# mLSTM mixer of a streaming encoder: normalisers as rows from 32-wide column tiles, the four old-state products of a head in one group, query copy ahead of decay

## The chip, the cores and the metric

One Trainium2 chip, one of its cores. TensorE (PE) multiplies, with its weight loads shown apart as PEld; VectorE (DVE) and ScalarE (ACT) work on what it leaves in PSUM; GpSimd (POOL) helps; SyncE (SP) issues the transfers. The metric is the device time of one execution in microseconds (us). The kernel before takes 1802.03 us, median of 3 runs (1801.32 to 1802.08).

## The reference, cut to what matters

Four layers, mLSTM, stick-breaking attention, latent attention, mLSTM, each followed by a squared-ReLU MLP; 256 prompt tokens and 32 sample tokens go through together. Only the two mLSTM mixers are touched. For each of four heads of width 512:

```python
b = jnp.cumsum(lf, axis=-1)
dmat = jnp.where(causal, b[..., :, None] - b[..., None, :] + li[..., None, :], -jnp.inf)
m_t = jnp.maximum(inter, jnp.max(dmat, axis=-1))            # inter = b + m
s = jnp.einsum('bhtd,bhsd->bhts', q, k) * jnp.exp(dmat - m_t[..., None])
num = w_inter[..., None] * jnp.einsum('bhtd,bhde->bhte', q, C) + jnp.einsum('bhts,bhse->bhte', s, v)
nq = w_inter * jnp.einsum('bhtd,bhd->bht', q, n) + jnp.sum(s, axis=-1)
h = num / jnp.maximum(jnp.abs(nq), jnp.exp(-m_t))[..., None]
C_new = g_state[..., None, None] * C + jnp.einsum('bhs,bhsd,bhse->bhde', g_tok, k, v)
n_new = g_state[..., None] * n + jnp.einsum('bhs,bhsd->bhd', g_tok, k)
```

The prompt has no history (C, n and m are zero); the sample starts from stored C, n and m. Outputs are h, through a layer norm per head, a gate and a down-projection, and C_new, n_new, m_new of both groups.

## The kernel before, in words

Every dense product is fp32 accuracy in three passes of a rounded part and a remainder (HH/HL, XGH/XGL, WHI/WLO); these stream through TensorE from the first to the last layer. Between the query/key/value projections and the down-projection of an mLSTM layer stands `mlstm_mix`, written out by hand for each engine, with a loop over the heads `h` and semaphores between the engines. Each engine does its instructions in the order written. PS is PSUM with 8 banks of 512 columns.

TensorE, head h: the value products (VTOK, PT) into banks 4 and 5, their sums (ONES, PT) into bank 7; for h > 0 the scores of the next head (QT, KT, into bank 1), the broadcast of its running maximum (R, SEL, into bank 6) and the second two old-state products of the head before (`old_state(h - 1, 2)`: KGH, VREP, 32 rows of the array each, banks 3 and 2); the sample's share of the head before (`sample`: QCP, I4); the sample's product with the stored state (QT, C0, bank 2), after which ACT copies bank 2 to QCP; four blocks of the prompt's new state (`new_state(b)`: KG, VTOK, banks 3 and 2 in turn); the normalisers (`columns`, below); `turn` (transposes of NB), `keys(h + 1)` (transposes of KT and KSC) and the first two old-state products of this head (`old_state(h, 0)`).

`columns` makes n_new in columns: four products of a 128-wide block of KS with one column of ones, and one of KGH with HB4 (four columns that mark the 32-token groups), all into bank 7. DVE adds the stored n, from COLS, into NOUT; at the end of the layer PE transposes NOUT once, ACT copies it to NST and SP stores p_n and s_n.

DVE, head h: `spread` (statistics of the layer norm, ends with hvar_out), `state(h - 1, 2)` (decay of the stored C and addition of the old-state products, L1344), `centre` (NB), `decay(h + 1)` (the argument DT), `columns`, `probs(h + 1)`, `outputs` (QT, L1379 and L1384), `keys(h + 1)` (KG, KGH, KS), `remainders` (HL, L1390), `state(h, 0)`. ACT, head h: reciprocal root, exponential of DT (`decay`, L799), the copy to QCP (L825), four copies to CPST (L806), the rounded part HH of the head (L837).

SP, one queue in written order: for each head the four stores of CPST to p_C, then, when DVE has finished both pairs of the head, the store of C0 to s_C (1 MB). For the last head a 512 KB weight tile of the down-projection stands between the s_C store of head 2 and the p_C stores of head 3.

After head 3 the sample's own result (NSB, its transposes, QT, HH, HL) has to be done before the down-projection starts; its remainder ends with smh_lo. `ready(k)` holds what the k-th step of the down-projection waits for: k = 0 takes the last head's first old-state pair and smh_lo, k = 2 the second pair.

Of the kernel before, what the change touches and what calls it, by code (L numbers as in the profile page):

```python
# [14 lines left out]
TP, TS = 256, 32  # L15
# [94 lines left out]
def hybrid_trunk_kernel(nc, d, o):  # L110

    ctx = ExitStack()
    with ctx:
# [35 lines left out]
        HB4 = at("HB4", [P, 4], take(16))  # L149
# [5 lines left out]
        NOUT = at("NOUT", [P, 2, AB], take(128))  # L155
# [29 lines left out]
        NST = at("NST", [32, P], take(512))  # L185
# [6 lines left out]
        PT_ = at("PT_", [P, 384], oa + 5120 + 4 * MLW)  # L192
        MASKM = at("MASKM", [P, MLW], o_raw + 3 * 4096 + 2048)
# [78 lines left out]
        def sem(name):  # L272
# [38 lines left out]
        cvs_done, cvs_out, cvs_dma, nst_done, nst_out, nst_dma, m_out, m_dma = [  # L311
            sem(n) for n in ("cvs_done", "cvs_out", "cvs_dma", "nst_done", "nst_out", "nst_dma", "m_out", "m_dma")]
# [49 lines left out]
        def new_bank(h, b):  # L362
            return 3 - b % 2 if h < AH - 1 else (6, 3, 2, 6)[b]

# [7 lines left out]
        def _(sp):  # L372
# [56 lines left out]
            for i in range(DEPTH):  # L429
                if i % 3 == 0:  # L430
# [40 lines left out]
                    dma(SEL[:], d["const_sel"], sel_in)  # L471
                    dma(C0[:, 0], d["state_mlstm_C"][la, 0, 0].rearrange("(b p) e -> p b e", p=P), c0_in[0])
# [4 lines left out]
                    dma(C0[:, 1], d["state_mlstm_C"][la, 0, 1].rearrange("(b p) e -> p b e", p=P), c0_in[1])  # L477
                    sp.wait_ge(m_out, la + 1)
                    dma(o["p_m"][la, 0].rearrange("(h a) -> h a", a=1), SMALL[:, 6:7], m_dma)
                    dma(o["s_m"][la, 0].rearrange("(h a) -> h a", a=1), SMALL[:, 7:8], m_dma)  # L480
                    for h in range(AH):
                        U = AH * la + h
                        if h == AH - 1:
                            sp.wait_ge(kxp_done, AH * (la + 1))
                            down_tile(3)
                        for b in range(4):
# [3 lines left out]
                            if b == 1 and 1 <= h < AH - 1:  # L490
# [9 lines left out]
                    sp.wait_ge(nst_out, la + 1)  # L500
                    dma(o["p_n"][la, 0].rearrange("h (b f) -> (h b) f", f=P), NST[0:16, :], nst_dma)
                    dma(o["s_n"][la, 0].rearrange("h (b f) -> (h b) f", f=P), NST[16:32, :], nst_dma)
# [84 lines left out]
            for s, n in ((y_dma, 80), (b_dma, 64), (c_dma, 64), (cvs_dma, 64), (nst_dma, 64), (m_dma, 64),  # L587
                         (cp_dma[0], 256), (cp_dma[1], 256), (cs_dma[0], 64), (cs_dma[1], 64)):
                sp.wait_ge(s, n)
# [45 lines left out]
        def _(act):  # L635
# [131 lines left out]
            def mlstm_mix(i, la):  # L767
# [50 lines left out]
                for h in range(AH):  # L818
                    U = AH * la + h
                    rsqrt(U, 2, hvar_out, hy_out)  # L820
                    if h + 1 < AH:
                        decay(h + 1)
# [3 lines left out]
                                   scale=AECOL[:, 12 + h:13 + h]).then_inc(qcp_out, 1)  # L826
                    for b in range(4):
# [3 lines left out]
                    if h == AH - 1:  # L831
                        act.wait_ge(nst_done, la + 1)
                        act.activation(NST[:], PS[0:32, 0, 0:P], ACT.Copy).then_inc(nst_out, 1)
# [210 lines left out]
        def _(dve):  # L1044
# [73 lines left out]
            dve.reduce_sum(HB4[:], IDENT[:].rearrange("p (j c) -> p j c", j=4), AX_X)  # L1118
# [124 lines left out]
            def mlstm_mix(i, la, evac_last):  # L1243
# [94 lines left out]
                def state(h, b0):  # L1338

                    U = AH * la + h  # L1340
                    for b in (b0, b0 + 1):
                        dve.wait_ge(cs_done, 4 * U + b + 1)
                        bank = (3, 2)[b % 2] if h < AH - 1 else (6, 7, 4, 5)[b]
                        ins = dve.scalar_tensor_tensor(C0[:, h % 2, b, :], C0[:, h % 2, b, :], AECOL[:, 25 + h:26 + h],  # L1344
                                                       PS[:, bank, :], ALU.mult, ALU.add)
                    ins.then_inc(cs_out, 1)
# [6 lines left out]
                for h in range(AH):  # L1353
# [11 lines left out]
                    def columns():  # L1365

                        dve.wait_ge(n_done, U + 1)
                        dve.tensor_copy(NOUT[:, 0, H4], PS[:, 7, 8:12])
                        n0 = cols_s(la) + N0 + 4 * h
                        dve.scalar_tensor_tensor(NOUT[:, 1, H4], COLS[:, n0:n0 + 4], AECOL[:, 25 + h:26 + h],  # L1370
# [1249 lines left out]
```

## Time and profile before

| | us |
|---|---|
| median of 3 runs | 1802.03 (1801.32 to 1802.08) |
| the profiled execution | 1799.49 |
| its span | 1797.3 |
| PE busy | 1762.9 (98% of the span) |
| DVE busy | 1142.1 (64%) |
| ACT busy | 876.2 (49%) |
| POOL busy | 160.4 (9%) |
| a head, from its value products to the next head's | 20.83 |

The span runs from the first to the last instruction. Busy PE is streaming, with weight loads beside it; one product in fp32 shows as two records. The two mLSTM mixers stand at 201 to 303 us and at 1429 to 1531 us of the span.

### The profile page before, as it was taken

How to read it: one execution, taken by the hardware profiler on the slowest of the kernel's cores; microseconds unless marked ns; L12 is line 12 of the kernel's file. 1: busy time of each engine (PE TensorE's matmuls, PEld its weight loads, DVE VectorE, ACT ScalarE, POOL GpSimd, SP SyncE). 2: the span in 40 equal slices, each digit the busy share in tenths (PEclk: the TensorE clock that was granted, in tenths of full speed). 3: DMA queues.
4: the chain of work that ended last, by engine and by line, in shares of the span. 5: the costliest groups of instructions: out<-in, count | busy, mean ns of one | idle time of the engine just before them, and what ended most of it. 6: DMA issues, size and time to landing. Idle time of an engine off the chain costs nothing.

```text
span 1797.3 us, 34006 instructions
## 1 busy us (share of the span) xinstructions
PE 1762.9 (98%) x13183; PEld 1641.1 (91%) x13183; DVE 1142.1 (64%) x1858; ACT 876.2 (49%) x1472; POOL 160.4 (9%) x111
## 2 busy tenths in 40 slices
PE   7999999999999999999999899999999999999998
PEld 6999855999999989999998699999999965999998
DVE  5886577575556546664575676554887567666544
ACT  4565422455444375554444555544665432455543
POOL 0000132110011001000120020010100034110000
PEclk9999999999999999999999999999999999999999
DMA  5565334555555624555544155555565424555553
GB/s 163 164 168 168 97 118 164 191 162 164 171 167 166 189 68 144 164 164 172 167 117 124 35 159 170 165 162 167 155 177 171 151 76 160 185 160 172 165 169 103
DMA packets 156171, 272.94 MB, mean 152 GB/s; under 512 B 22725, under 2 KB 28306, under 8 KB 156058
## 3 DMA queue, kind: packets, MB, share of 16 engines
q1 hardware_dynamic: 156058, 271.37, 48.6%
q8 instruction: 79, 1.29, 0.3%
q14 instruction: 34, 0.28, 0.1%
HBM read 250.55 MB, written 20.78 MB: 151 GB/s over the span
## 4 chain that ended last, share of the span: by engine, by line
PE 88%; DVE 8%; ACT 3%; DMA 1%; issue 1%; SPq 0%; DVEq 0%; ACTq 0%
PE PS L1796 86%; PE PS L1801 2%; ACT PB L960 1%; DVE C L1344 1%; DVE WLO L1067 1%; DVE QT L1379 0%; DVE NB L1335 0%; DMA out_p_C_dram<-CPST 0%; DMA RAWT<-in_c_w_ukv_dram 0%; DMA XIN<-in_x_sample_dram 0%; DVE TMP L1654 0%; DVE QT L1384 0%; DVE BST L1321 0%; DVE KS L1311 0%; DVE HL L1390 0%
## 5 line engine op out<-in xcount | busy, mean ns | idle before, releaser
L1067 DVE TENSOR_TENSOR WLO<-RAWT,WHI 128x512 fp32r<-128x512 f32 (+1 forms) x904 | 635.6, 720 | 481.7 <-ACT WHI L658 479.7
L658 ACT ACTIVATE WHI<-RAWT 128x512 fp32r<-128x512 f32 (+1 forms) x904 | 555.1, 626 | 648.2 <-PE PS L1796 645.6
L1796 PE MATMUL PS<-XGH,WHI 128*128 128x288 f32 x1776 | 526.7, 297 | 4.7 <-DVE WLO L1067 4.0
L1796 PE MATMUL PS<-HH,WHI 128*128 128x288 f32 (+1 forms) x1792 | 528.8, 295 | 0.4 <-issue 0.4
L1796 PE MATMUL PS<-HH,WLO 128*128 128x288 f32 (+1 forms) x1792 | 527.5, 294 | 0.0
L1796 PE MATMUL PS<-HL,WHI 128*128 128x288 f32 (+1 forms) x1792 | 527.1, 294 | 0.0
L1796 PE MATMUL PS<-XGH,WLO 128*128 128x288 f32 x1776 | 523.7, 295 | 0.0
L1796 PE MATMUL PS<-XGL,WHI 128*128 128x288 f32 x1776 | 523.4, 295 | 0.0
L1796 PEld LDWEIGHTS PS<-XGH,WHI 128*128 128x128 f32 x1776 | 333.9, 188 | 8.3 <-DVE WLO L1067 4.8
L1796 PEld LDWEIGHTS PS<-HH,WHI 128*128 128x128 f32 x1792 | 336.5, 188 | 3.9 <-issue 3.6
L1796 PEld LDWEIGHTS PS<-HH,WLO 128*128 128x128 f32 x1792 | 336.6, 188 | 0.0
L1796 PEld LDWEIGHTS PS<-HL,WHI 128*128 128x128 f32 x1792 | 336.5, 188 | 0.0
L1796 PEld LDWEIGHTS PS<-XGL,WHI 128*128 128x128 f32 x1776 | 333.8, 188 | 0.2
L1796 PEld LDWEIGHTS PS<-XGH,WLO 128*128 128x128 f32 x1776 | 333.7, 188 | 0.2
L1720 POOL TENSOR_TENSOR SQ<-X 128x1152 f32<-128x1152 f32 x13 | 32.8, 2522 | 892.7 <-DVE X L1079 544.9
L1796 PE MATMUL PS<-VTOK,KG 128*128 128x512 f32 x128 | 60.8, 605 | 0.8 <-ACT QCP L825 0.8
L1010 ACT ACTIVATE TMP<-TMP 128x1152 f32<-128x1152 f32 x32 | 37.4, 1169 | 23.2 <-DVE TMP L1654 23.2
L1654 DVE SCALAR_TENSOR_TENSOR TMP<-PS,RSTD 128x1152 f32<-128x1152 f32 x32 | 43.5, 1358 | 6.2 <-PE PS L1796 6.0
L1796 PEld LDWEIGHTS PS<-VTOK,KG 128*128 128x128 f32 x128 | 22.2, 190 | 26.1 <-issue 24.9
L1663 DVE TENSOR_TENSOR HL<-TMP,HH 128x1152 f32 (+1 forms) x32 | 43.2, 1351 | 2.9 <-ACT HH L1012 2.9
L1152 DVE SCALAR_TENSOR_TENSOR CV__90<-TMPX,COLS,CV__90 128x291 f32<-128x291 f32 x96 | 43.5, 516 | 2.1 <-ACT CV__90 L733 2.1
L672 ACT ACTIVATE XGH<-X,COLS 128x288 fp32r<-128x288 f32 x64 | 29.1, 525 | 23.5 <-DVE X L1124 12.8
(364 smaller groups left out, 1420.1 us busy)
## 6 DMA issues: line engine op xcount, KB each, us to landing
RAWT<-in_w_ff_dram SPq DMA_DIRECT2D x256, 512.0 KB, 3.7
RAWT<-in_a_w_up_dram SPq DMA_DIRECT2D x64, 512.0 KB, 3.7
RAWT<-in_a_w_down_dram SPq DMA_DIRECT2D x32, 512.0 KB, 3.6
RAWT<-in_b_w_qkv_dram SPq DMA_DIRECT2D x24, 512.0 KB, 3.8
RAWT<-in_a_w_q_dram SPq DMA_DIRECT2D x16, 512.0 KB, 3.7
RAWT<-in_a_w_k_dram SPq DMA_DIRECT2D x16, 512.0 KB, 3.6
RAWT<-in_a_w_v_dram SPq DMA_DIRECT2D x16, 512.0 KB, 3.7
C<-in_state_mlstm_C_dram SPq DMA_DIRECT2D x8, 1024.0 KB, 5.9
```

The source lines that it names most:

```text
L658: act.activation(hi, raw, ACT.Copy).then_inc(weight_hi, 1)
L672: ins = act.activation(XGH[:, f, :], X[:, f, :], ACT.Copy, scale=COLS[:, gain(nu) + f:gain(nu) + f + 1])
L960: ins = act.activation(PB[:, p % 3, a, k0:k0 + n], PS[:, b0 + a, k0:k0 + n], ACT.Exp, bias=c[:, 1, a, x:x + 1], scale=CVQ[:, 4, x:x + 1], ...
L1010: act.activation(TMP[:], TMP[:], ACT.Square).then_inc(h_sq, 1)
L1067: dve.tensor_tensor(lo, raw, hi, ALU.subtract).then_inc(weight_lo, 1)
L1152: ins = dve.scalar_tensor_tensor(CV_[:, a, 0:291], TMPX[:, a, j:j + 291], COLS[:, w0:w0 + 1], CV_[:, a, 0:291], ALU.mult, ALU.add)
L1344: ins = dve.scalar_tensor_tensor(C0[:, h % 2, b, :], C0[:, h % 2, b, :], AECOL[:, 25 + h:26 + h], PS[:, bank, :], ALU.mult, ALU.add)
L1654: dve.scalar_tensor_tensor(TMP[:], PS[:, 4 * b:4 * b + 4, 0:T], 0.0, over4(RSTD[:]), ALU.max, ALU.mult).then_inc(group_out, 1)
L1663: dve.tensor_tensor(HL[:, bass.ds(4 * g, 4), :], TMP[:], HH[:, bass.ds(4 * g, 4), :].bitcast(F32), ALU.subtract).then_inc(h_lo, 1)
L1720: link(pool.tensor_tensor(SQ[:], x, x, ALU.mult))
L1796: return pe.matmul(out, lhsT, rhs, start=start, stop=stop, **kw)
L1801: return pe.transpose(out, in_, IDENT[0:n, 0:n])
```

## The change

Three edits, and the moves that they need.

1. `columns` makes n_new in rows. Per head four products with ONES as 32-wide stationary side and a 128-wide block of KS moving, each into its own 32 partitions of bank 7, and four with BLOCKS (ones for one 32-token group) and KGH. DVE copies one 128x128 block (NROWP) and combines the other with the stored n (NROWS<-N0R,AECOL,PS). The stored n comes as rows, spread over 32 partitions each, by four transfers for each head (`old_n`), and p_n and s_n are stored for each head. The transpose, NST and HB4 go.
2. The four old-state products of a head stand in one group, behind the next head's value products, in banks 1, 6, 2, 3; what writes these banks waits for the DVE step that reads them. In the last head they stand at k = 2 of the down-projection, and `new_state(0)` behind the sample's products.
3. ACT copies the query product (QCP) ahead of the exponential of the decay. DVE's `remainders` run one head late, ahead of `outputs`; those of head 2 come after the `centre` of NSB.

```diff
@@ banks, and the order on SP @@
+        def old_bank(h, b):
+            return ((1, 6, 2, 3) if h < AH - 1 else (6, 7, 4, 5))[b]
...
+                    def old_n(h):
+                        rows_ = d["state_mlstm_n"][la, 0, h].rearrange("(b f) -> b f", f=P)
+                        for b in range(4):
+                            dma(N0R[TS * b:TS * (b + 1)], rows_[b:b + 1].to_broadcast([TS, P]), n0_in)
...
                         if h == AH - 1:
                             sp.wait_ge(kxp_done, AH * (la + 1))
                             down_tile(3)
+                        if h:
+                            sp.wait_ge(n_out, U)
+                            old_n(h)
...
+                        sp.wait_ge(n_out, U + 1)
+                        for row, name in ((NROWP, "p_n"), (NROWS, "s_n")):
+                            dma(o[name][la, 0, h].rearrange("(b f) -> b f", f=P),
+                                row[0:P:TS, :], nst_dma)
...
-                        sp.wait_ge(cs_out, 2 * U + 2)
+                        sp.wait_ge(cs_out, 4 * U + 4)
                         dma(o["s_C"][la, 0, h].rearrange("(b p) e -> p b e", p=P), C0[:, h % 2], cs_dma[h % 2])
@@ ACT, mlstm_mix @@
                     rsqrt(U, 2, hvar_out, hy_out)
-                    if h + 1 < AH:
-                        decay(h + 1)
                     act.wait_ge(qc_done, U + 1)
...
+                    if h + 1 < AH:
+                        decay(h + 1)
@@ DVE, columns and the order of a head @@
                         dve.wait_ge(n_done, U + 1)
-                        dve.tensor_copy(NOUT[:, 0, H4], PS[:, 7, 8:12])
...
+                        if U:
+                            dve.wait_ge(nst_dma, 32 * U)
+                        dve.wait_ge(n0_in, 64 * (U + 1))
+                        dve.tensor_copy(NROWP[:], PS[:, 7, P:2 * P])
+                        dve.scalar_tensor_tensor(NROWS[:], N0R[:], AECOL[:, 25 + h:26 + h],
+                                                 PS[:, 7, 2 * P:3 * P], ALU.mult, ALU.add).then_inc(n_out, 1)
...
                         probs(h + 1)
+                        if h:
+                            remainders(h - 1)
                         outputs()
                         keys(h + 1)
-                        remainders()
                         state(h, 0)
...
                 columns()
                 dve.wait_ge(sy_out, la + 1)
                 centre([PS[:, 0, :]], [NSB[:]], 1, sn_out)
+                remainders(AH - 2)
                 dve.wait_ge(sxp_done, la + 1)
@@ PE, a head @@
                     if h:
-                        if not last:
-                            scores(h + 1, (0,))
-                            broadcast(h + 1)
-                        if last:
-                            new_state(0)
-                        pe.wait_ge(cs_out, 2 * U - 1)
-                        old_state(h - 1, 2)
+                        pe.wait_ge(cp_out, 4 * U)
+                        old_state(h - 1)
+                        sample(h - 1)
...
+                        else:
+                            pe.wait_ge(cs_out, 4 * U - 3)
+                            scores(h + 1, (0,))
+                            pe.wait_ge(cs_out, 4 * U - 2)
+                        broadcast(h + 1)
                         scores(h + 1, (1,))
                         if h:
-                            sample(h - 1)
-                            pe.wait_ge(cs_out, 2 * U)
+                            pe.wait_ge(cs_out, 4 * U)
...
                         for b in range(4):
-                            mm(PS[:, 7, 8 + b:9 + b], KS[:, b * P:(b + 1) * P], ONES[:, 0:1])
-                        mm(PS[:, 7, 12:16], KGH[:, h % 2, :], HB4[:]).then_inc(n_done, 1)
+                            mm(PS[32 * b:32 * b + 32, 7, P:2 * P], ONES[:, 0:TS], KS[:, b * P:(b + 1) * P])
+                        for b in range(4):
+                            ins = mm(PS[32 * b:32 * b + 32, 7, 2 * P:3 * P], BLOCKS[:, b, :], KGH[:, h % 2, :])
+                        ins.then_inc(n_done, 1)
...
@@ PE, start of the down-projection @@
                         if k == 0:
-                            last_state(0)
-                            pe.wait_ge(nst_out, la + 1)
                             pe.wait_ge(smh_lo, la + 1)
                         if k == 2:
-                            last_state(2)
+                            last_state()
```

On PE, head 1 of the first mLSTM layer before, from its value products on (VREP,KGH are old-state products, QCP,I the sample's share of the head before, C,QT the product with the stored state, VTOK,KG the new state):

```order
L1796 MATMUL PS<-VTOK,PT__104 128x512 [waits hg_out,prob_out]
L1796 MATMUL PS<-ONES,PT__104 128x1 [waits kg_out]
L1796 MATMUL PS<-QT,KT 128x256 x4
L1796 MATMUL PS<-R,SEL 128x288
L1796 MATMUL PS<-VREP,KGH 128x512 [waits cs_out]
L1796 MATMUL PS<-QCP,I 32x512 [waits qcp_out]
L1796 MATMUL PS<-C_109,QT 32x512 [waits c0_in1,cs_out]
```

And the same place now:

```order
L1814 MATMUL PS<-VTOK,PT__102 128x512 [waits hg_out,prob_out]
L1814 MATMUL PS<-ONES,PT__102 128x1 [waits kg_out]
L1814 MATMUL PS<-VREP,KGH 128x512 [waits cp_out]
L1814 MATMUL PS<-VREP,KGH 128x512 x3
L1814 MATMUL PS<-QCP,I 32x512 [waits qcp_out]
L1814 MATMUL PS<-QT,KT 128x256 [waits cs_out]
L1814 MATMUL PS<-R,SEL 128x288 [waits cs_out]
L1814 MATMUL PS<-C_110,QT 32x512 [waits c0_in1,cs_out]
```

All four old-state products now stand ahead of the next head's scores, and the scores, the broadcast and the product with the stored state each wait for a DVE step that reads them.

On SP, the first mLSTM layer before, from the s_C store of head 2 on (C and C_109 are the same tile):

```order
L374 DMA out_s_C_dram<-C_109 128x4x512 [waits cs_out]
L374 DMA RAWT<-in_a_w_down_dram 128x2x512 [waits weight_lo_ready,kxp_done]
L374 DMA out_p_C_dram<-CPST 128x512 [waits cp_out] x4
L374 DMA RAWT<-in_a_w_down_dram 128x2x512 [waits weight_lo_ready] x4
L374 DMA out_s_C_dram<-C_109 128x4x512 [waits cs_out]
```

And now (N0R are the rows of the stored n of head 3):

```order
L378 DMA out_s_C_dram<-C_110 128x4x512 [waits cs_out]
L378 DMA RAWT<-in_a_w_down_dram 128x2x512 [waits weight_lo_ready,kxp_done]
L378 DMA N0R<-in_state_mlstm_n_dram 32x128 [waits n_out]
L378 DMA N0R<-in_state_mlstm_n_dram 32x128 x3
L378 DMA out_p_C_dram<-CPST 128x512 [waits cp_out] x4
L378 DMA out_p_n_dram<-NROWP 4x128 [waits n_out]
```

The four row loads of head 3 stand behind the 1 MB store and the 512 KB weight tile, in the same queue.

## Rows read from the trace of the kernel before

**Rows 1.** Chain that ended last, share of the span by engine

```profile
PE 88%; DVE 8%; ACT 3%; DMA 1%; issue 1%; SPq 0%; DVEq 0%; ACTq 0%
```

**Rows 2.** Timeline, PE, head 2, first layer: start us, us, instruction, count [idle before]

```profile
260.61 2.84 PE L1796 MATMUL PS<-VTOK,PT__104 128*128 128x512 f32 x6
263.88 1.97 PE L1796 MATMUL PS<-QT,KT 128*128 128x256 f32 x8
265.78 0.51 PE L1796 MATMUL PS<-R,SEL 4*128 4x288 f32 x1
...
268.99 1.06 PE L1796 MATMUL PS<-C,QT 128*32 128x512 f32 x8
...
271.81 0.95 PE L1796 MATMUL PS<-ONES,KS 128*128 128x1 f32 x8
...
273.18 3.70 PE L1796 MATMUL PS<-VTOK,KG 128*128 128x512 f32 x8 [0.20 <-ACT QCP L825]
...
280.38 1.13 PE L1796 MATMUL PS<-VREP,KGH 32*128 32x512 f32 x4
281.44 1.13 PE L1796 MATMUL PS<-VTOK,PT__104 128*128 128x512 f32 x2
```

**Rows 3.** Timeline, PE, head 0, first layer

```profile
225.80 0.75 PE L1796 MATMUL PS<-R,SEL 4*128 4x288 f32 x2
...
230.51 0.95 PE L1796 MATMUL PS<-ONES,KS 128*128 128x1 f32 x8
...
231.54 0.68 PE L1796 MATMUL PS<-VTOK,KG 128*128 128x512 f32 x1
```

**Rows 4.** Timeline, DVE, heads 1 to 2, first layer

```profile
262.57 1.21 DVE L1390 TENSOR_TENSOR HL<-QT,HH 128x1024 fp32r<-128x1024 f32 x1
263.71 1.39 DVE L1344 SCALAR_TENSOR_TENSOR C<-C,AECOL,PS 128x512 f32<-128x512 f32 x2
265.02 0.15 DVE L1317 SCALAR_TENSOR_TENSOR LNS<-PS,AECOL 128x2 f32<-128x2 f32 x1
...
267.54 1.40 DVE L1344 SCALAR_TENSOR_TENSOR C<-C,AECOL,PS 128x512 f32<-128x512 f32 x2
...
277.79 0.48 DVE L1379 SCALAR_TENSOR_TENSOR QT<-PS,COLS,SX 128x256 f32<-128x256 f32 x1 [3.79 <-PE PS L1801]
```

**Rows 5.** Timeline, PE, head 3 and start of the down-projection, both layers

```profile
303.22 0.37 PE L1796 MATMUL PS<-HH,WHI 128*128 128x288 f32 x1 [0.22 <-issue]
...
1510.09 2.84 PE L1796 MATMUL PS<-VTOK,PT__104 128*128 128x512 f32 x6
...
1531.09 0.37 PE L1796 MATMUL PS<-HH,WHI 128*128 128x288 f32 x1 [0.22 <-issue]
```

**Rows 6.** Timeline, DVE, end of head 3, second layer

```profile
1524.28 0.21 DVE L1370 SCALAR_TENSOR_TENSOR NOUT<-COLS,AECOL,PS 128x4 f32<-128x4 f32 x1
...
1525.29 0.81 DVE L1335 TENSOR_SCALAR NSB<-PS,MV,LNS 128x512 f32<-128x512 f32 x1
1527.29 0.69 DVE L1415 TENSOR_TENSOR QT<-PS,COLS 128x512 f32<-128x512 f32 x1 [1.19 <-PE PS L1801]
```

**Rows 7.** Timeline, SP's queue: five mask loads, and head 3 of the second layer

```profile
196.41 2.20 SPq L374 DMA_DIRECT2D MASKM<-in_const_mask_ml_dram  x5
...
1519.58 0.38 SPq L374 DMA_DIRECT2D out_s_C_dram<-C  x1
1520.07 0.45 SPq L374 DMA_DIRECT2D RAWT<-in_a_w_down_dram  x1
```

**Rows 8.** DMA issues of 1519 to 1521 us: count, KB, us to landing

```profile
RAWT<-in_a_w_down_dram SPq DMA_DIRECT2D x1, 512.0 KB, 5.8
out_p_C_dram<-CPST SPq DMA_DIRECT2D x1, 256.0 KB, 5.9
```

**Rows 9.** Timeline, PE, latent attention

```profile
958.07 1.17 PE L1796 MATMUL PS<-QRW,PERM 32*32 32x288 f32 x16 [1.89 <-DVE QR L1521]
```

**Rows 10.** Windows: stretch, length, busy us of PE, PEld, DVE, ACT, POOL, granted clock, DMA

```profile
959.00:964.00 5.00, 5.00 (x31) 4.70 (x27) 2.40 (x5) 0.10 (x1) 0.00 (x0) 0.66 0.34 105
```

More of the change, by code:

```diff
@@ L184, in hybrid_trunk_kernel @@
         SX = at("SX", [P, 4, T], o_tmp)
-        NST = at("NST", [32, P], take(512))
+        BLOCKS = at("BLOCKS", [P, 4, TS], take(512))
         VT_ = at("VT_", [P, AB, T], o_h + 16 * BLK)
@@ L192, in hybrid_trunk_kernel @@
         PT_ = at("PT_", [P, 384], oa + 5120 + 4 * MLW)
+        N0R = at("N0R", [P, P], oa + 5120 + 4 * MLW + 1536)
+        NROWP = at("NROWP", [P, P], oa + 5120 + 4 * MLW + 2048)
+        NROWS = at("NROWS", [P, P], oa + 5120 + 4 * MLW + 2560)
         MASKM = at("MASKM", [P, MLW], o_raw + 3 * 4096 + 2048)
@@ L585, in _ @@
             dma(o["y_sample"][0], YO[YSAMPLE, 2], y_dma)
[L587 removed]
+            for s, n in ((y_dma, 80), (b_dma, 64), (c_dma, 64), (cvs_dma, 64), (nst_dma, 256), (m_dma, 64),
                          (cp_dma[0], 256), (cp_dma[1], 256), (cs_dma[0], 64), (cs_dma[1], 64)):
@@ L1342, in state @@
                         dve.wait_ge(cs_done, 4 * U + b + 1)
[L1343 to L1346, printed above, removed]
+                        dve.scalar_tensor_tensor(C0[:, h % 2, b, :], C0[:, h % 2, b, :], AECOL[:, 25 + h:26 + h],
+                                                 PS[:, old_bank(h, b), :], ALU.mult, ALU.add).then_inc(cs_out, 1)
                 decay(0)
@@ L1422, in mlstm_mix @@
                 outputs()
-                remainders()
+                remainders(AH - 1)
                 def last_state():
@@ L1726, in squares @@
                     pool.tensor_tensor(SSUM[:, 1, :], SSUM[:, 0, :], SQ[:, 0, :], ALU.add).then_inc(ssum, 1)
+            link(pool.memset(BLOCKS[:], 0.0))
+            for b in range(4):
+                link(pool.memset(BLOCKS[TS * b:TS * (b + 1), b, :], 1.0))
             pool.wait_ge(cols_out, 2)
@@ L2035, in broadcast, with old_state @@
                     mm(PS[:, 6 if h else 4, 0:T], SEL[:, h, :], R[:, 0:T]).then_inc(bcast_done, 1)
-                def old_state(h, b0):
-                    U = AH * la + h
+                def old_state(h):
                     vh = slice(512 * h, 512 * (h + 1))
-                    for b in (b0, b0 + 1):
+                    for b in range(4):
                         r = slice(32 * b, 32 * b + 32)
-                        bank = (3, 2)[b % 2] if h < AH - 1 else (6, 7, 4, 5)[b]
-                        mm(PS[:, bank, :], KGH[r, h % 2, :], VREP[r, vh]).then_inc(cs_done, 1)
+                        mm(PS[:, old_bank(h, b), :], KGH[r, h % 2, :], VREP[r, vh]).then_inc(cs_done, 1)
                 scores(0)
@@ L2109, in mlstm_mix @@
                                skip_group_check=True)
+                        pe.wait_ge(cs_out, 4 * U - 2)
+                        new_state(0)
                     else:
```

47 lines of the change are left out of this document (16 added, 31 removed).

## The prediction, made before the changed kernel ran

> **What bounds the kernel now.** I read the page first: its chain of waits is 88% PE and 8% DVE [rows 1], so a change counts by what it does to PE's sequence, and where PE waits, by what DVE does. Then the timeline of PE in the mixer. A head takes 281.44 - 260.61 = 20.83 us from its value products to the next head's [rows 2], and PE sits idle in it for 0.20 us only, ahead of `new_state(1)`, for ACT's copy to QCP. The timeline of DVE shows where the two meet. The first old-state pair is taken up at 263.71, 3.10 us after the head's start N; `spread` takes 267.54 - 265.02 = 2.52 us, and the second pair ends at 267.54 + 1.40 = 268.94 [rows 4]. PE's product with the stored state starts at 268.99, N + 8.38 [rows 2]: this place already goes by DVE. Later DVE idles for 3.79 us ahead of `outputs` [rows 4]. Last the end of the mixer: from N of head 3 to the first down-projection product 303.22 - 281.44 = 21.78 us in the first layer and 1531.09 - 1510.09 = 21.00 us in the second [rows 2, 5]. I number what follows from N of each head.
>
> **Normalisers as rows, heads 0 to 2.** Before, eight records of one moving column and two of four take 231.54 - 230.51 = 1.03 us where nothing waits [rows 3]; the weight loads of 128 columns set that pace. Now there are eight products of 128 columns in 32-wide tiles. The nearest row is the product with the stored state, eight records of 512 columns in the same kind of tiles in 1.06 us [rows 2]: four tiles run side by side. A quarter of its columns gives 0.25 us, twice 0.5 us, and I add 0.13 us for getting in and out of the tiles: 0.63 us. The bounds are 0.4 us and, if the tiles took turns, 16 records of some 0.11 us, 1.8 us. So -0.40 us in head 0. In heads 1 and 2 the stretch from the first normaliser record to `new_state(1)` is 273.18 - 271.81 = 1.37 us with the idle 0.20 us [rows 2]; with QCP copied earlier that wait goes and 0.63 us stay: -0.74 us.
>
> The page TensorEngine Tiling (Array Packing) of the Trainium skill, section Tiling Modes, speaks against this edit: a change of tiling mode drains the engine. No run here isolates that drain; the sum has 0.13 us for it, and it would have to be 0.53 us before the edit gained nothing in head 0.
>
> **The four old-state products.** The pair at the end of a head goes from there: 281.44 - 280.38 = 1.06 us [rows 2]. In head 0 that is a plain gain, as is the group's absence in it. Head 0 gives -1.06 - 0.40 = -1.46 us.
>
> In heads 1 and 2 the group stands behind the value products and their sums, 263.88 - 260.61 = 3.27 us [rows 2]. Two products on 32 rows each take 1.06 us; I take four, on four different row groups and banks, for the same time. DVE then sees the first at N + 3.36 + 1.13 + 0.04 = N + 4.5 instead of N + 3.1. Its order is unchanged: a pair 265.02 - 263.71 = 1.31 us, `spread` 2.52 us, a pair 1.40 us [rows 4], so it ends at N + 9.8. PE meanwhile does group, sample product, scores, the broadcast by itself (0.75 us [rows 3], no longer beside an old-state pair) and the rest of the scores, and is there at about N + 9.2. So it waits 0.6 us, and the product with the stored state starts at N + 9.8, not N + 8.38. What follows it was 281.44 - 268.99 = 12.45 us [rows 2] and is 12.45 - 1.06 - 0.74 = 10.65 us. The new head takes 20.45 us: -0.38 us each. Much of the second edit is paid back here by DVE.
>
> **What DVE takes on in a head.** Two operations of 128 columns for two of 4 (about +0.3 us), the row loads, and `remainders` ahead of `outputs` (1.14 us from start to start [rows 4]). All of it lies in the 3.79 us before `outputs`. The rows of heads 1 and 2 are queued behind the s_C store of the head before, which leaves at N + 9.8; they should land by N + 15 and at the latest 6.3 us later, N + 16.1, as the tile behind such a store did (0.49 + 5.8 us [rows 7, 8]). DVE is through at N + 17.2, or N + 18.4 at the latest, and `outputs` has its input at N + 17.9. If this cover fails, each us later costs some 0.5 to 1 us per head.
>
> **The last head.** Here the loads show. The group starts after the small sums too, N + 3.6; DVE takes it up at N + 4.75 and not N + 3.1, so s_C of head 2, in the second layer 1519.58 - 1510.09 = N + 9.49 before [rows 5, 7], leaves at N + 11.1. The weight tile follows 0.49 us later, then the four loads at the pace of the mask loads, 2.20 / 5 = 0.44 us each [rows 7]. They are issued by N + 13.4, but the queue is full: the tile landed 0.49 + 5.8 = 6.3 us after the store's issue, and the p_C store behind the tile at least 1520.52 + 5.9 - 1519.58 = 6.8 us after it [rows 7, 8]. I take 6.4 us, near the tile, since the rows are 64 KB: N + 17.5. DVE reaches `columns` at about N + 15.8 (1524.28 [rows 6] is N + 14.2, and 1.65 us later) and stands until then. Behind it wait the centring of NSB, then `remainders` of head 2, then the sample's QT. From NOUT's start to the end of NSB is 1525.29 + 0.81 - 1524.28 = 1.82 us [rows 6], 1.6 us without NOUT; so QT starts at 17.5 + 0.5 + 1.6 + 1.14 = N + 20.75. Before it was at 1527.29, N + 17.20, with 1.19 us idle, and the down-projection started 1531.09 - 1527.29 = 3.80 us later [rows 5, 6]; without the NST copy on ACT I take 3.6 us. The start is N + 24.35: +2.57 us in the first layer, +3.35 us in the second.
>
> Sum: 2 x (-1.46 - 2 x 0.38) + 2.57 + 3.35 = -4.44 + 5.92 = +1.5 us.
>
> **The clock.** PE now pauses for about 3 us ahead of the NSB transposes and again for about 2 us ahead of the down-projection, with some 2 us of work between. In the latent attention it paused for 1.89 us and did 32-wide products [rows 9], and then over 959 to 964 us the granted clock was 0.66 of full on the mean [rows 10], so part of it was at the lower of the two levels, 1.2 GHz. Full work there lost (1 - 0.66) x 5 = 1.7 us. In either tail that could happen at the dense start of the down-projection; part of the slow stretch will fall on PE's own waits, and I take 1.7 us for both layers together. Bounds are 0 and 3.4 us. The Trainium skill says of this, on the page TensorE: Matmul & The Clock Gate, section Why this matters for your kernels, that bursts of products should follow one another without pauses or the clock goes back to half; the rows agree as far as they go.
>
> The remaining edits cost nothing I can price: the fills of BLOCKS run on POOL at the start, where PE waits for its first input; p_n and s_n leave in stretches in which the queue is free; the old group at k = 2 of the down-projection takes the place of a pair.
>
> Total +1.5 + 1.7 = +3.2 us. The sum is on the profiled execution, 1799.49 us, which stands 2.54 us under the median 1802.03: 1802.7 us for such an execution, and 1805.2 us as the median.
>
> **Rivals.**
>
> A, the rows come in time. Then `columns` in head 3 runs at about N + 15.8 and no long pause arises. QT starts 1.7 us earlier, the start of the down-projection is at N + 22.6: 2 x 22.6 - 42.78 - 4.44 = -2.0 us; with the 0.2 to 0.5 us per head that DVE's small operations and the tiles may save beyond my figures, about -3 us, 1799.0 us. For it: the loads are small and issued by N + 13.4. Against it: one queue, and 1.5 MB ahead of them. Chance 0.16. The Trainium skill's page DMA: Bandwidth & Descriptors, section Anatomy of one DMA, fits a transfer as 2.0 us plus its bytes over 436 GB/s; by that the 16 KB of the last load would be there about 2.04 us after its issue, at N + 15.4, which is this rival. The row of the tile, 5.8 us for 512 KB, shows waiting that this fit leaves out.
>
> B, the clock falls in both tails and costs its whole price: 1.5 + 2 x 1.7 = +4.9 us, 1806.9 us. It decides once PE's pauses in head 3 pass 1.89 us each. For it: the pauses I compute are longer than the one that did it. Against: the stretch between them is dense. Chance 0.27.
>
> C, the four old-state products do not run side by side and take 2.12 us. Then PE comes to the product with the stored state at N + 10.3, not N + 9.2: +0.5 us in heads 1 and 2 each, and +1.06 us at k = 2, 2.06 us a layer. On top of my sum that is 3.2 + 4.1 = +7.3 us, 1809.3 us. For it: nothing in the trace shows more than two of these at once. Against: four column tiles do it. Chance 0.12.
>
> **How the numbers follow.** My forecast has 0.45. A measurement of this kernel tells 0.2%, 3.6 us, from no change, so under 1798.4 is faster and over 1805.6 slower. Faster: half of A and a little of the rest, 0.12. Slower: B and C and a little of the forecast, 0.40. The rest is within, 0.48. The range takes A below and most of C above: 1798.0 to 1809.0 us.
>
> **What would show it.** In the profile after: the wait of PE for DVE's C operation ahead of the product with the stored state, about 0.6 us in heads 1 and 2; the normaliser records close to 0.63 us; four VREP,KGH products in little over 1.06 us; DVE idle for a transfer to N0R ahead of NROWP in head 3 and not before `outputs` in other heads; PE idle about 3 us ahead of the NSB transposes; the clock row of the first us of the down-projection. I would be wrong if DVE never waits for N0R, if the group takes 2 us, or if heads 1 and 2 gain the full 1 us of the moved pair.

## The result, and the profile after

| | median | runs | ratio to before, 95% interval |
|---|---|---|---|
| before, in the same comparison | 1799.63 us | 13 | |
| changed | 1806.97 us | 13 | 1.0047 [1.0038, 1.0056] |

The change makes the kernel slower, by 0.47% or 8.5 us (the two medians are 7.3 us apart; where nothing else is said, I turn ratios into us). The profiled execution took 1812.97 us (span 1811.1 us, mean granted clock 0.990); it is one of three above 1811 us, and the other ten lie between 1804.44 and 1808.11 us. I had forecast +3.2 us on 1802.03 us. The kernel before came out 2.4 us lower in these runs than in the three known then, so the forecast time, 1805.2 us, looks better than the forecast difference.

The chain of waits still is nearly all PE, and a transfer has come into it:

```profile
PE 90%; DVE 6%; ACT 2%; DMA 1%; issue 1%; SPq 0%; DVEq 0%; ACTq 0%
PE PS L1814 88%; PE PS L1819 2%; DVE C L1355 1%; DVE WLO L1080 1%; DMA N0R<-in_state_mlstm_n_dram 0%; SPq L378 0%; DVE BST L1333 0%; ACT PB L973 0%; DMA XIN<-in_x_sample_dram 0%; DVE TMP L1669 0%; DVE NT L1105 0%; DVE NT L1106 0%; ACT NY L695 0%; ACT NY L696 0%; ACT CV__88 L748 0%
```

As in the prediction, N is the start of a head's value products. Head 2 on PE, against [rows 2] (start, length, instruction, count, idle before in brackets):

```profile
258.35 2.74 PE L1814 MATMUL PS<-VTOK,PT__102 128*128 128x512 f32 x6
260.92 0.72 PE L1814 MATMUL PS<-ONES,PT__102 128*128 128x1 f32 x6
261.58 1.14 PE L1814 MATMUL PS<-VREP,KGH 32*128 32x512 f32 x8
262.65 1.04 PE L1814 MATMUL PS<-QCP,I 128*32 128x512 f32 x2
...
268.04 1.06 PE L1814 MATMUL PS<-C,QT 128*32 128x512 f32 x8 [0.42 <-DVE C L1355]
269.04 1.98 PE L1814 MATMUL PS<-VTOK,KG 128*128 128x512 f32 x4
270.95 0.42 PE L1814 MATMUL PS<-KS,ONES 128*32 128x128 f32 x8
271.19 0.40 PE L1814 MATMUL PS<-KGH,BLOCKS 128*32 128x128 f32 x8
271.52 3.70 PE L1814 MATMUL PS<-VTOK,KG 128*128 128x512 f32 x8
...
278.64 0.59 PE L1814 MATMUL PS<-VTOK,PT__102 128*128 128x512 f32 x1
```

The head takes 278.64 - 258.35 = 20.29 us, 0.54 us less than before. The four old-state products need 262.65 - 261.58 = 1.07 us, the time of two before. The normalisers need 271.52 - 270.95 = 0.57 us. The idle time moved from ACT's QCP to DVE's C.

On DVE, `columns` waits for the rows in every head. In heads 1 and 2 of the first layer that is inside the slack ahead of `outputs`, which shrinks from 3.79 [rows 4] to 0.58 us. In the second layer DVE waits longer there, 3.73 and 3.42 us, nothing is left of the slack, and the two heads take 20.49 and 20.57 us instead of 20.29. In head 3 nothing covers the wait:

```profile
252.89 0.29 DVE L1381 COPY NROWP<-PS 128x128 f32<-128x128 f32 x1 [2.17 <-DMA N0R<-in_state_mlstm_n_dram]
...
276.14 1.66 DVE L1391 SCALAR_TENSOR_TENSOR QT<-PS,COLS,SX 128x256 f32<-128x256 f32 x4 [0.58 <-PE PS L1819]
...
297.08 0.29 DVE L1381 COPY NROWP<-PS 128x128 f32<-128x128 f32 x1 [3.13 <-DMA N0R<-in_state_mlstm_n_dram]
...
298.32 0.81 DVE L1347 TENSOR_SCALAR NSB<-PS,MV,LNS 128x512 f32<-128x512 f32 x1
299.04 1.22 DVE L1403 TENSOR_TENSOR HL<-QT,HH 128x1024 fp32r<-128x1024 f32 x1
300.18 0.68 DVE L1430 TENSOR_TENSOR QT<-PS,COLS 128x512 f32<-128x512 f32 x1
```

SP's queue shows why (head 3 starts at 278.64), and the DMA issues of 289 to 296 us add size and median time to landing:

```profile
289.53 0.38 SPq L378 DMA_DIRECT2D out_s_C_dram<-C  x1
290.03 0.44 SPq L378 DMA_DIRECT2D RAWT<-in_a_w_down_dram  x1
290.51 2.91 SPq L378 DMA_DIRECT2D N0R<-in_state_mlstm_n_dram  x4
```

```profile
out_s_C_dram<-C SPq DMA_DIRECT2D x1, 1024.0 KB, 5.1
RAWT<-in_a_w_down_dram SPq DMA_DIRECT2D x1, 512.0 KB, 6.0
N0R<-in_state_mlstm_n_dram SPq DMA_DIRECT2D x4, 16.0 KB, 4.3
```

Transfers of 16 KB take 4.3 us behind 1.5 MB. PE's end of the mixer, first and second layer, against [rows 5]:

```profile
299.18 0.66 PE L1819 MATMUL PS<-IDENT,NSB 128*128 128x128 f32 x4 [3.61 <-DVE NSB L1347]
299.67 1.88 PE L1814 MATMUL PS<-VTOK,KG 128*128 128x512 f32 x4
303.91 0.37 PE L1814 MATMUL PS<-HH,WHI 128*128 128x288 f32 x1 [2.35 <-issue]
...
1534.24 1.11 PE L1819 MATMUL PS<-IDENT,NSB 128*128 128x128 f32 x4 [3.86 <-DVE NSB L1347]
1535.15 3.62 PE L1814 MATMUL PS<-VTOK,KG 128*128 128x512 f32 x4
1540.86 0.58 PE L1814 MATMUL PS<-HH,WHI 128*128 128x288 f32 x1 [2.09 <-issue]
```

In the second layer the same four new-state records take 3.62 us instead of 1.88 us: TensorE is at 1.2 GHz. The windows around both places, with the granted clock ahead of DMA share and GB/s:

```profile
304.00:308.00 4.00, 4.00 (x19) 4.00 (x20) 2.84 (x6) 1.44 (x2) 0.00 (x0) 0.57 0.38 134
1533.00:1547.00 14.00, 10.67 (x36) 7.81 (x38) 10.21 (x16) 2.70 (x5) 0.00 (x0) 0.51 0.21 76
```

The clock stays low into the down-projection, but it falls in a different place in either layer. In the first, the transposes of NSB and the products between the two pauses still have their full-clock lengths, and the granted clock falls behind the second pause, with the down-projection under way (1.00 in 303 to 304 us, 0.70 in the next microsecond, 0.50 from 305). In the second it falls while PE still waits for NSB (1.00 in 1532 to 1533 us, 0.60 in the next, 0.50 from 1534): the transposes already take 1.11 us instead of 0.66.

The 13.8 us between the two profiled spans come from the same operations of VectorE found in both traces: 2.0 us in the first mixer and the start of its down-projection, 7.3 us in the second, 3.1 us in the latent attention (low clock near 1000 to 1024 us here, near 960 us before) and 1.4 us in small pieces. The latent attention's share differs from run to run, and this execution is one of the slowest; the difference over all runs, 8.5 us by the ratio, needs the experiments.

### The profile page after: what moved, and what is told of

The parts are those of the page before. It is cut to its first block, busy times and chain, and to the rows that moved or that the text cites. A ratio compares the mean times of both kernels' runs of the same rounds, so it can differ in the third digit from the quotient of the medians.

```text
span 1811.1 us, 34152 instructions
## 1 busy us (share of the span) xinstructions
PE 1767.8 (98%) x13229; PEld 1641.1 (91%) x13229; DVE 1144.3 (63%) x1857; ACT 877.6 (48%) x1470; POOL 155.2 (9%) x116
## 4 chain that ended last, share of the span: by engine, by line
PE 90%; DVE 6%; ACT 2%; DMA 1%; issue 1%; SPq 0%; DVEq 0%; ACTq 0%
PE PS L1814 88%; PE PS L1819 2%; DVE C L1355 1%; DVE WLO L1080 1%; DMA N0R<-in_state_mlstm_n_dram 0%; SPq L378 0%; DVE BST L1333 0%; ACT PB L973 0%; DMA XIN<-in_x_sample_dram 0%; DVE TMP L1669 0%; DVE NT L1105 0%; DVE NT L1106 0%; ACT NY L695 0%; ACT NY L696 0%; ACT CV__88 L748 0%
## 5 line engine op out<-in xcount | busy, mean ns | idle before, releaser
L821 ACT ACTIVATE CPST<-PS 128x512 f32<-128x512 f32 x32 | 19.1, 595 | 49.1 <-PE PS L1814 43.1
```

The costliest lines, as they stand in the source:

```text
L821: act.activation(CPST[:, q % 2, :], PS[:, new_bank(q // 4 % AH, q % 4), :], ACT.Copy).then_inc(cp_out, 1)
```

## The experiments

I read two things of each: the ratio to the runs of before made beside it, and "lost to the clock", the mean over its runs of (1 - mean granted clock) x span. The latter counts time of the low clock in which PE waits too, so it is a guide and no exact share. Every span ends in a stretch at the low level, so none comes to zero.

| kernel | median us | runs | before beside it | ratio, 95% interval | lost to the clock, us (before) |
|---|---|---|---|---|---|
| changed | 1806.97 | 13 | 1799.63 | 1.0047 [1.0038, 1.0056] | 10.4 |
| rows_early | 1796.43 | 12 | 1800.29 | 0.9990 [0.9975, 1.0005] | 6.4 (3.6) |
| cols_old | 1796.60 | 12 | 1800.29 | 0.9985 [0.9976, 0.9994] | 2.5 (3.6) |
| early_pause | 1804.80 | 6 | 1800.29 | 1.0037 [1.0023, 1.0052] | 12.0 (3.6) |
| before_pause | 1805.24 | 6 | 1797.25 | 1.0053 [1.0034, 1.0071] | 6.0 (2.5) |
| filler | 1798.95 | 12 | 1800.29 | 1.0002 [0.9990, 1.0015] | 3.0 (3.6) |
| fill_a | 1805.21 | 12 | 1798.76 | 1.0030 [1.0018, 1.0042] | 8.6 (3.2) |
| fill_b | 1803.38 | 12 | 1798.76 | 1.0029 [1.0016, 1.0041] | 6.6 (3.2) |
| early_fill | 1793.49 | 11 | 1797.25 | 0.9982 [0.9972, 0.9991] | 2.4 (2.5) |
| fill_cols | 1792.40 | 12 | 1797.25 | 0.9972 [0.9961, 0.9983] | 3.3 (2.5) |
| cols_first | 1792.13 | 7 | 1798.76 | 0.9961 [0.9943, 0.9979] | 5.1 (3.2) |

Read from their PE timelines, from each head's first value product to the next one's, and for head 3 to the down-projection:

| kernel | heads 1 and 2 | head 3, layer 1 | head 3, layer 2 |
|---|---|---|---|
| before | 20.83 | 21.78 | 21.00 |
| changed | 20.29 (20.49, 20.57 in layer 2) | 25.27 | 27.61 |
| filler | 20.29 | 25.16 | 24.96 |
| rows_early | 20.29 | 22.20 | 22.22 |
| cols_old | 20.63 | 23.60 | 22.38 |
| decay_first | 20.99 | 22.20 | 22.36 |
| rem_late | 20.29 | 21.94 | 21.94 |
| cols_first | 19.52 | 21.94 | 21.96 |

### The rows asked for earlier: rows_early

```diff
-                        if h:
-                            sp.wait_ge(n_out, U)
-                            old_n(h)
...
                             dma(o[name][la, 0, h].rearrange("(b f) -> b f", f=P),
                                 row[0:P:TS, :], nst_dma)
+                        if h < AH - 1:
+                            old_n(h + 1)
```

> The changed kernel, but SyncE asks for the stored-n rows of head h+1 right behind the p_n and s_n stores of head h, so ahead of that head's s_C store (1 MB) and, for head 3, ahead of the weight tile. Nothing else differs. Theory (the wait for N0R in the last head is the loss): VectorE's wait of 3.13 us ahead of NROWP in the last head goes in both layers, the down-projection starts 3.1 us earlier each time, 6.2 us in all, and more where the clock no longer falls behind the pause: 1797 to 1801, at or under the kernel before. Rival (the four products in one group, and the feature order around them, are the loss): the sample's chain through QCP, NSB and the remainders still ends late, and no more than 2 us comes back: 1805 or more.

The loss is gone. On SP the loads now leave ahead of the s_C store, and PE's two waits at the end are these:

```profile
280.73 1.83 SPq L378 DMA_DIRECT2D N0R<-in_state_mlstm_n_dram  x4
290.31 0.41 SPq L378 DMA_DIRECT2D out_s_C_dram<-C  x1
```

```profile
296.87 0.66 PE L1818 MATMUL PS<-IDENT,NSB 128*128 128x128 f32 x4 [0.52 <-DVE NSB L1346]
301.60 0.37 PE L1813 MATMUL PS<-HH,WHI 128*128 128x288 f32 x1 [2.35 <-issue]
```

The start comes at N + 22.2 instead of N + 25.3, 3.1 us earlier, as expected. From 1.0047 to 0.9990 is 10 us, more than 2 x 3.1 us. The rival falls. That the kernel is then faster than before isn't shown: the interval reaches 1.0005.

### Part 1 undone: cols_old

```diff
-    mm(PS[32 * b:32 * b + 32, 7, P:2 * P], ONES[:, 0:TS], KS[:, b * P:(b + 1) * P])
+    mm(PS[:, 7, 8 + b:9 + b], KS[:, b * P:(b + 1) * P], ONES[:, 0:1])
...
-    dve.wait_ge(n0_in, 64 * (U + 1))
-    dve.tensor_copy(NROWP[:], PS[:, 7, P:2 * P])
+    dve.tensor_copy(NOUT[:, 0, H4], PS[:, 7, 8:12])
```

> The changed kernel with part 1 undone: the normalisers come as columns again (four products with one moving column of ONES and one with HB4), NOUT is transposed at the end, no rows are loaded or stored for each head; the one group of old-state products, the query copy and the late remainders stay. Theory (rows of N0R are the loss): without them the last head ends as early as with early rows, less 0.4 us a head for the dearer column products: 1799 to 1802. Rival (the grouping is the loss): 1805 or more, as the changed kernel.

1796.6 us, a little better than expected. The group, the query copy and the late remainders by themselves are a gain of 0.15%, 2.7 us; all of the loss is in part 1. The rows are nevertheless right in themselves: a head takes 20.63 us here and 20.29 us with them.

### The wait without the transfer: early_pause and before_pause

```diff
                 dve.wait_ge(sy_out, la + 1)
+                for x in range(8):
+                    link(dve.tensor_copy(PT_[:], DT[:, 0:384]))
                 centre([PS[:, 0, :]], [NSB[:]], 1, sn_out)
```

> The kernel with early rows (rows_early), and at the very place where VectorE waited for N0R in the last head eight chained copies of 128x384 ahead of the centring of NSB, roughly 3 us, with no transfer in them. Theory (only the wait in that place counts, however it comes about): the loss comes back whole, 1805 to 1809. Rival (the loss is in what the late transfers do to the queue, not in the wait): it stays near rows_early, within 2 us.

> The kernel before, with eight chained copies of 128x384 on VectorE ahead of the centring of NSB in the last head of both layers (3.2 us, as early_pause showed), all else as before. Theory (a pause of TensorE in this place costs its own length and then a stretch at 1.2 GHz, whatever the normalisers and the grouping are): 2 x 3.2 = 6.4 us of waiting less at most 1.2 us that the NSB path has in hand, plus 4 to 8 us of clock: 1809 to 1814. Rival (the clock answers to the changed order of the head, not to the pause): 1804 to 1807, the waiting alone.

In early_pause PE waits 3.68 us for NSB, with no late transfer anywhere, and the ratio is 1.0037. It lies just under the changed kernel's interval (from 1.0038), the two intervals overlap, and it is far from the 0.9990 of rows_early. The wait is what counts, not what the transfers do to each other. In before_pause the pause is 2.5 us:

```profile
1534.98 0.66 PE L1803 MATMUL PS<-IDENT,NSB 128*128 128x128 f32 x4 [2.51 <-DVE NSB L1335]
1539.48 0.37 PE L1798 MATMUL PS<-HH,WHI 128*128 128x288 f32 x1 [0.22 <-issue]
```

The down-projection starts 23.73 - 21.00 = 2.73 us later in the layer whose clock stayed full, 5.5 us for both. The median is 8.0 us over the 1797.25 us beside it, the ratio 9.5 us, 6.1 to 12.8 us. The waiting alone lies just below that interval, so a pause costs more than its length in the old order as well: by about 4 us going by the ratio, the lower end of what I expected, and by 2.5 us going by the medians. In the first layer of this execution the low clock is there: the same four new-state records that take 1.88 us at full clock take 3.30 us behind the pause. As a time, 1805.24 us lies in the rival's range and not in mine; both ranges were set on a before of some 1800 us, and taken down by those 3 us they leave it between them, nearer to mine. The excess is small beside the interval.

### The pauses filled: filler, fill_a and fill_b

These keep the waits for data and give TensorE transposes of IDENT to do meanwhile, whose results are overwritten. The filler kernel has both edits, fill_a the first alone, fill_b the second alone.

```diff
                 new_state(2)
+                for x in range(24):
+                    xp(PS[:, 1, 0:P], IDENT[:])
                 pe.wait_ge(sn_out, la + 1)
...
                 pe.wait_ge(cp_out, 4 * U + 3)
+                for x in range(14):
+                    xp(PS[:, 2, 0:P], IDENT[:])
                 return last_state
```

> The changed kernel with 24 extra 128x128 transposes of IDENT on TensorE ahead of the NSB transposes and 14 ahead of the down-projection, in the last head of both layers, at places where it waits 3.6 and 2.4 us; their results are overwritten. The waits for data stay as long as they were. Theory (part of the loss is TensorE's clock falling behind these pauses): stretches at 1.2 GHz at the start of the down-projection go, and the time falls by 2 to 6 us, to 1801 to 1805. Rival (the clock's stretches come from elsewhere and the pauses alone cost): no change, 1807, or up to 1 us more where the extra transposes run over the wait.

> The changed kernel with only the first of the two fillings: 24 extra 128x128 transposes of IDENT where TensorE waits 3.6 us for NSB in the last head; the second pause (2.4 us ahead of the down-projection) stays empty. Theory (the clock falls because of the long pause that the rows caused): most of what filler gained (8.0 us, from 1807.0 to 1799.0) comes here, 1799 to 1802. Rival (the two pauses count only together, or the second one decides): 1804 or more.

> The changed kernel with only the second filling: 14 extra transposes ahead of the down-projection, where TensorE waits 2.4 us; the pause of 3.6 us for NSB stays empty. Theory (the long pause that the rows caused is the one the clock answers to): 1804 to 1807. Rival (the second pause decides, which the kernel before does not have): 1799 to 1802.

In filler the down-projection of the first layer starts as late as in the changed kernel, at N + 25.16, yet the time is back at that of before, lower than the 1801 to 1805 us that I expected:

```profile
295.56 2.78 PE L1819 MATMUL PS<-IDENT 128*128 128x128 f32 x24
299.32 0.66 PE L1819 MATMUL PS<-IDENT,NSB 128*128 128x128 f32 x4 [0.98 <-DVE NSB L1347]
301.54 1.69 PE L1819 MATMUL PS<-IDENT 128*128 128x128 f32 x14
303.94 0.37 PE L1814 MATMUL PS<-HH,WHI 128*128 128x288 f32 x1 [0.71 <-issue]
```

The windows of the two starts of the down-projection have the full clock:

```profile
304.00:308.00 4.00, 4.00 (x32) 3.42 (x32) 2.84 (x6) 1.30 (x2) 0.00 (x0) 1.00 0.43 138
1529.00:1543.00 14.00, 13.89 (x103) 13.01 (x104) 11.49 (x19) 5.26 (x8) 0.00 (x0) 1.00 0.46 140
```

In four microseconds PE does 32 records here, 19 in the changed kernel. So most of the loss was clock: 1.0047 to 1.0002 is 8.1 us. The Trainium skill's rule that products should follow one another without pauses (TensorE: Matmul & The Clock Gate, Why this matters for your kernels) agrees with filler, even for products that compute nothing. My guess that the first, longer pause decides was wrong: each filling alone gives 0.17 to 0.18%, 3 us, and both give 8 us. Whether that is more than the sum, 6.3 us, the intervals don't tell.

The two profiles, of one execution each, show how one filling can fall short. With the first pause filled but for 0.97 and 2.11 us (fill_a), both layers reach the down-projection at full clock, and it falls there, behind the second pause: 0.50 in 305 to 307 us and in 1534 to 1536 us. With the second filled (fill_b), the first layer keeps the full clock; in the second PE waits 4.74 us for NSB, and the transposes behind that take 1.11 us. So a pause of 2.35 us can be enough, and the longer one can be too, but neither did it every time.

### ACT's order undone: decay_first

```diff
+                    if h + 1 < AH:
+                        decay(h + 1)
                     act.wait_ge(qc_done, U + 1)
...
-                    if h + 1 < AH:
-                        decay(h + 1)
```

> rows_early with ACT's query copy put back behind the exponential of the decay. Theory of the prediction (0.20 us of TensorE's idle time a head came from that order): the wait of the new state's second product for QCP comes back, about 0.2 us or a little less in heads 1 and 2, and the head cycle is 20.3 to 20.5 us instead of 20.29. Rival: since TensorE reaches this product later than before (at N+9.7 instead of N+8.4), the exponential is long done and no wait comes back: cycle 20.29.

Neither was right. The wait comes back three times as long as it was before the change [rows 2], and the head takes 20.99 us, 0.70 us more:

```profile
270.43 0.40 PE L1813 MATMUL PS<-KGH,BLOCKS 128*32 128x128 f32 x8
271.46 3.70 PE L1813 MATMUL PS<-VTOK,KG 128*128 128x512 f32 x8 [0.63 <-ACT QCP L839]
```

```profile
270.28 0.55 ACT L813 ACTIVATE DT<-DT 128x416 f32<-128x416 f32 x1 [3.89 <-DVE DT L1294]
270.74 0.67 ACT L839 ACTIVATE QCP<-PS,AECOL 128x512 f32<-128x512 f32 x1
```

ACT stands 3.89 us for DVE's DT, and the query product was done 2.0 us before that wait ended. With DT that late, the order on ACT is worth more than the 0.20 us that I had read off the old order. That makes up 2.8 us in four heads. It was one run; the cycle is read from its trace, and its time decides nothing.

### The remainders of head 2: rem_late

```diff
-                remainders(AH - 2)
                 dve.wait_ge(sxp_done, la + 1)
...
                    .then_inc(smh_lo, 1)
+                remainders(AH - 2)
                 outputs()
```

> rows_early with the remainders of head 2 (1.22 us on VectorE) behind the sample's in the last head instead of behind NSB. By the prediction they cost their length, 1.14 us, on the path to the down-projection: its start would be at N+21.1 instead of N+22.2. Rival: they run while VectorE would wait for the transposes of NSB anyway (1.19 us in the kernel before), so that the start moves by 0.3 us or less, to N+21.9.

```profile
295.23 0.81 DVE L1346 TENSOR_SCALAR NSB<-PS,MV,LNS 128x512 f32<-128x512 f32 x1
296.79 0.69 DVE L1428 TENSOR_TENSOR QT<-PS,COLS 128x512 f32<-128x512 f32 x1 [0.75 <-PE PS L1818]
```

The start moves to N + 21.94, by 0.26 us: the rival is right. VectorE has to wait for the transposes of NSB anyway, here 0.75 us, and the 1.22 us stood mostly in that wait. It is one run, 1800.95 us, at a mean clock of 0.994; its time decides nothing.

### Towards a better kernel: early_fill, fill_cols, cols_first

The early_fill kernel is rows_early with 3 and 17 of the extra transposes. The cols_first kernel is rem_late with this, and fill_cols is both together:

```diff
                         if h:
+                            pe.wait_ge(hvar_out, U + 1)
+                            columns()
                             pe.wait_ge(cs_out, 4 * U)
...
-                        columns()
+                        if h == 0:
+                            columns()
```

> rows_early (1796.4 us, mean clock 0.9964) with the extra 128x128 transposes of IDENT on TensorE: 3 ahead of the NSB transposes and 17 ahead of the down-projection, in the last head of both layers, so that its pauses of 0.5 and 2.35 us there are filled. Theory (the loss has two parts that add: the wait for the rows, which rows_early removes, and the low clock behind the pauses, which filler removed): the clock loss falls from 6.4 to 2 to 3 us and the time to 1791 to 1794. Rival (the clock gain of filler came by chance of the runs, or needs the longer pause): 1796 to 1798, as rows_early.

> early_fill, and in heads 1 and 2 the normaliser products stand ahead of the product with the stored state, where TensorE waits 0.42 us for VectorE's C (and in the last head remainders of head 2 come behind the sample's). Theory: the products (0.57 us) fit into the 0.42 us wait, the head cycle falls from 20.29 to 19.9 us, 4 heads by 0.4 = 1.6 us, and nothing else is late: 1789.5 to 1792.5. Rival: the new state's second product then waits for ACT's QCP, since only 0.92 us of other products is left to cover it, and gives half or all of it back: within 0.5 us of early_fill.

> fill_cols without its extra transposes: early rows, normaliser products ahead of the product with the stored state in heads 1 and 2, remainders of head 2 behind the sample's. The pause of 2.35 us ahead of the down-projection is empty again. If that pause costs clock, as early_fill (1793.5) against rows_early (1796.4) says: 1794 to 1796.5. If fill_cols needed no filling: 1791 to 1793.

The early_fill kernel lost less to the clock than rows_early (2.4 and 6.4 us), but the ratios, 0.9982 and 0.9990, overlap: a gain in time from filling this 2.35 us pause isn't shown. The profiles point to one: the start of the down-projection has the full clock in both layers of early_fill, while in rows_early it is at 0.50 in 302 to 305 us, behind this pause and one of 0.52 us. In cols_first PE runs through:

```profile
265.75 0.22 PE L1813 MATMUL PS<-COLS,QT 128*32 128x1 f32 x8
265.81 0.41 PE L1813 MATMUL PS<-KS,ONES 128*32 128x128 f32 x8
266.03 0.40 PE L1813 MATMUL PS<-KGH,BLOCKS 128*32 128x128 f32 x8
266.38 1.07 PE L1813 MATMUL PS<-C,QT 128*32 128x512 f32 x8
267.38 5.42 PE L1813 MATMUL PS<-VTOK,KG 128*128 128x512 f32 x12
```

The normalisers fill the wait for C, no wait for QCP appears in heads 1 and 2, and the head takes 19.52 us, 0.77 us less where I expected 0.4. In four heads that is 3.1 us. The fill_cols kernel shows only 1.1 us of it against early_fill in the same comparison; its down-projection waits 0.62 us once more in each layer for WLO, the remainder of a weight tile, since the remainders now stand in VectorE's way there, and it lost 0.9 us more to the clock. The cols_first kernel, without any filling, has the lowest time: 1792.13 us, 0.9961 [0.9943, 0.9979], 7 us under the kernel before; its interval overlaps that of fill_cols. My expectation that it needed the filling was wrong.

## Why the prediction was right and wrong

**Normalisers, old-state group, heads.** Right. 0.57 us for 0.63, 1.07 us for four products where I took 1.06, so rival C falls. Head 0 takes 19.33 us: -1.42 and -1.50 us for -1.46. The product with the stored state starts at N + 9.69, with a wait of 0.42 us, for N + 9.8 and 0.6. Heads 1 and 2 gain 0.54 us for 0.38 where the rows come in time. The 3.79 us ahead of `outputs` were to cover the row loads there; in the second layer of the profiled execution they didn't quite, which cost 0.20 and 0.28 us.

**The query copy.** In the sum as the 0.20 us idle of the old order. It is worth 0.70 us a head in the new one (decay_first). The forecast cycle held, since I had worked it out for the new order; only the price put on this edit was too small.

**The last head.** Right in its mechanism, short in one term. The loads left at N + 11.87, close to N + 11.6. Their four issues took 2.91 us and not 4 x 0.44 = 1.8 us, and DVE had the last row at N + 18.44, not N + 17.5. The rest followed in the steps that I gave: from there to QT 300.18 - 297.08 = 3.10 us for 3.24, from QT to the down-projection 3.73 us for 3.6. So the start was N + 25.27 for N + 24.35. Only the remainders of head 2 were priced wrongly inside these steps: they stand there with 1.14 us, and rem_late shows that they lengthen the path by 0.26 us, since VectorE would mostly have waited. Rival A needed the rows in time; in its order they weren't, and in rows_early, where they are, the start is at N + 22.2 for the N + 22.6 of that rival. The rule by which it would have come out, 2.0 us plus bytes over bandwidth (the Trainium skill, DMA: Bandwidth & Descriptors, Anatomy of one DMA), gives an estimate of 2.04 us for 16 KB. The page states it for transfers on GpSimd's path, and these are issued by SP, so it was no sure ground for them. Here it was 4.3 us behind 1.5 MB, which the fit leaves out, and 1.8 us in rows_early with no megabyte right ahead, close to it.

**The sum of the waits.** With filler's numbers, which have the full clock, it is -1.42 - 2 x 0.54 + 3.38 = +0.88 us in the first layer and -1.50 - 2 x 0.54 + 3.96 = +1.38 us in the second: +2.3 us, forecast +1.5.

**The clock.** The term that was mis-sized. I took 1.7 us for both layers and 3.4 us as its upper bound. The measured difference less the waits is 8.5 - 2.3 = 6.2 us, and taking the low clock away brought 8.1 us. Rival B had the right mechanism, the clock falling in both tails, and its 1806.9 us is the closest time, by luck of the base, since its difference was +4.9 us. Its price per tail was carried over from one short stretch in the latent attention [rows 10]. That price occurs: in fill_a's profile 1 less the granted clock, summed over the single microseconds behind the second pause, gives 1.7 us in either layer. But it should have been open above: in the second layer of the changed kernel's profiled execution the mean granted clock is 0.51 over 14 us, and the transposes, the new-state products and the start of the down-projection ran at half rate through it. That execution is one of the three slowest, but early_pause's profile, at 1804.29 us, has a stretch at 0.50 from 1526 to 1538 us in the same place; how often it gets so long isn't shown. I had also counted on the products between the two pauses to hold the clock; in the first layer they didn't, and in the second it had fallen before them.

So +3.2 us was forecast and +8.5 us measured. Of the 5.3 us between, about 4.5 are the clock and 0.8 the waits.

## What to carry to other kernels

A wait put on a dense TensorE stretch has two prices, its length and what the clock takes afterwards; here the clock took 6 to 8 us beside the wait of some 3.1 us that the rows added in each of two layers. Give it an open upper bound, and test it by filling the pause with products that compute nothing. A small load costs what stands ahead of it in its queue: issue it as soon as its buffer is free, ahead of the megabyte. And look for work that can go into a wait, as the normalisers did here, before shortening anything.

## What the runs showed of the hardware

- Four products on 32 rows each, on four row groups and into four banks, take 1.07 us, as two did before; 128 columns in 32-wide column tiles, eight records, take some 0.24 us from start to start.
- TensorE at 1.2 GHz: four records of 128x512 in 3.62 us, at 2.4 GHz 1.88 us. With two pauses of 3.6 and 2.35 us and 1.9 us of products between, the clock fell behind the second in one layer; in the other it fell during a first pause of 3.86 us. The filling of either pause alone took away only about 3 of 8 us, and with the first filled (fill_a) the clock fell behind the second, of 2.35 us, in both layers.
- Four loads of 16 KB took 1.83 us to issue on SP and landed 1.8 us after it in rows_early, where two 256 KB stores and two of 2 KB stood ahead; behind 1.5 MB it was 2.91 and 4.3 us. Behind the 1 MB load of C in head 0 of the changed kernel the issue took 1.90 us and the landing 4.3 us, so the two times don't go together. Why is open.
- Open: why the low clock in the latent attention lies near 960 us in one execution, near 1000 us in another and is missing in a third (filler), though nothing in that part was changed.
